# Router by tiles with stationary weights, an earlier first gather, and a last expert loaded in parts, in a float32 decoder trunk on one Trainium2 core

## The chip, the cores and the metric

The kernel runs on one core of one Trainium2 chip. The metric is the time of one execution on the device in microseconds (us); lower is better. All data are float32.

## What is computed

```python
# x: (1, 256, 1024). Layer 0: sliding-window attention and a dense SwiGLU (D_FF 2816).
# Layer 1: pooling mixer, then 8 experts of 3584, of which each token uses 2.
x = x + sliding_window_attention(rms_norm(x, attn_norm), ...)
x = x + swiglu(rms_norm(x, ffn_norm), ffn_w_gate, ffn_w_up, ffn_w_down)
x = x + pooling_mixer(rms_norm(x, pool_norm), pool_w, pool_scale)
t = rms_norm(x, moe_norm)
logits = t @ w_router                       # (256, 8)
top_val, top_idx = lax.top_k(logits, 2)
gates = softmax(top_val)                    # combine[token, expert]
for e in range(8):
    out += combine[:, e:e+1] * ((silu(t @ w_gate[e]) * (t @ w_up[e])) @ w_down[e])
x = x + out
return rms_norm(x, final_norm)
```

## The kernel before, in words

The 256 tokens are two tiles `t` of 128. `xres` holds the residual, `nrm` its normalised copy. Each engine runs its own instruction list in order, and semaphores (`wait_ge`, `then_inc`) tie them together. All weights come through a ring of six SBUF slots of 28 KB per partition; SyncE (SP) issues the loads in order and waits ahead of each one until TensorE has read the slot's old content.

The order around the change is this.

1. **Pooling mixer.** TensorE runs `map_groups(t, half)` (L1281), VectorE adds its result to `xres` (`add_mix`, L832).
2. **Router.** TensorE transposes raw `xres` (`raw_transposes`, L1291) into banks 0 to 3, ScalarE copies these to `rT` (L577), and TensorE multiplies (`logits`, L1304): the 128x128 token block is stationary and only 8 columns, the experts, move. For each tile there are 8 products, which the profile shows as 16 matmul instructions. VectorE copies the logits (L852), takes the top two and builds `mask` (L858). TensorE turns the masks of both tiles into ranks, with `upper` and `ones` as the other operand (L1326 to L1332), VectorE makes `slot` from them (L862, L865) and compares with `iota_f` to get the selection matrix `disp` (`dispatch`, L874). `keep_busy(n)` (L1267) puts in transposes of the identity whose result nobody reads.
3. **First gather.** `gather(0, 0)` (L1335) selects the tokens of expert 0: 16 products of `nrm` by `disp`, 32 instructions, begun when `disp` is there for both tiles. VectorE's `keep_xg` (L880) multiplies the result by the gain, into `xg`.
4. **Flags.** From the counts VectorE ranks the experts by load and writes `flags` (L907 to L930), of which SP, TensorE, ScalarE and VectorE read which expert is next and whether it has over 64 tokens (`ext`, the overflow).
5. **Experts** (`expert`, L1438). Each has 12 chunks of 3.5 MB: gate and up in turns (c = 0 to 7, `gate_up`, L1411, overflow L1392), then four of down (c = 8 to 11, L1503, overflow L1524). The result `y` of an expert is scattered back to the tokens during the next one (`scatter`, L1367), and VectorE adds it to `xres` (L899).
6. **Final.** After expert 7 `final` scatters its `y`, behind a branch on `ext` (L1376: no overflow). ScalarE makes the sum of squares and the root (L507), VectorE multiplies by the gain `final_norm` (L1043, L1051) and by the reciprocal root (L1056, columns 0 to 511; ScalarE L646 has the others), and SP stores each tile (L434).

VectorE's order in the router is: `add_mix` of all halves, `norm(3, t)` (scaling of `nrm`, L657), top two of both tiles, `slot`, `dispatch(0, 0)`, the counts and flags, then `keep_xg(0, 0)`.

Of the kernel before, what the change touches and what calls it, by code (L numbers as in the profile page):

```python
# [20 lines left out]
P = 128  # L21
# [70 lines left out]
def trunk_kernel(nc, x, norm_gains, attn_w_qkv, attn_sinks, attn_w_o, ffn_w_gate, ffn_w_up,  # L92
                 ffn_w_down, pool_w, pool_scale, moe_w_router, moe_w_gate,
                 moe_w_up, moe_w_down, final_norm, out):
    with ExitStack() as ctx:
# [66 lines left out]

        upper = part(arena, 4096, P)
# [22 lines left out]
        lg = sb("lg", [P, T, NE])  # L186
# [22 lines left out]
        full = [sem(f"full{i}") for i in range(SLOTS)]  # L209
        pool_step = sem("pool_step")  # L210
# [39 lines left out]
        poolT_ready = sem("poolT_ready")  # L250
        router_ready = sem("router_ready")
# [3 lines left out]
        mix_done = sem("mix_done")  # L255
        logits_done = sem("logits_done")
# [34 lines left out]
        out_ready = sem("out_ready")  # L291
# [63 lines left out]

        def moe_full(it, c):


            return landed[moe_slot(c)] + 32 * it + 16 * (c // SLOTS + 1)
# [5 lines left out]
        def _(sp):  # L365
# [8 lines left out]
            def load_chunk(it, e, c):  # L374
# [5 lines left out]
                sp.dma_start(ring[s][:, :], w.rearrange("o p n -> (o p) n")).then_inc(full[s], 16)  # L380
# [51 lines left out]
            for t in range(T):  # L432
                sp.wait_ge(out_ready, 2 * t + 2)
                sp.dma_start(out[0].rearrange("(t p) d -> t p d", p=P)[t], out_rows(t)).then_inc(out_sent, 16)  # L434
# [5 lines left out]
        def _(pool):  # L440
# [19 lines left out]
            own.link(nc.gpsimd.tensor_copy(iota_f[:, :], iota_w[:, 0:CAP]))  # L460
# [22 lines left out]
            nc.gpsimd.memset(comb[:, :, NIT:NIT + 1], 0.0).then_inc(zeros_ready, 1)  # L483


            for done, n in ((y_ready, 2), (yx_ready, 2), (sc_ready, 1), (ctr_done, 1), (scat_done, 4), (xadd_done, 8)):
                pool.sem_inc(done, n)


        @block.scalar  # L490
        def _(act):
# [9 lines left out]
            def norm(q, t):  # L501

                if q == 0:
                    act.wait_ge(x_in[t], 16)
                else:
# [65 lines left out]
            for t in range(T):  # L571
                norm(2, t)
            for t in range(T):
                norm(3, t)
                for kh in range(2):
# [3 lines left out]
                                         ACT.Copy).then_inc(rT_ready, 1)  # L579
            preload(ACT.Exp)  # L580
# [56 lines left out]
            with act.If(over > 0):  # L637
                with act.Fori(NE, NIT, 1) as it:
                    expert(it)
            with act.Else():  # L640
                pass
            preload(ACT.Sqrt)
            for t in range(T):
                norm(4, t)
                act.wait_ge(rstd_ready, t + 1)
                nc.scalar.activation(out_rows(t)[:, BANK:D], out_rows(t)[:, BANK:D], ACT.Copy,  # L646
                                     scale=rstd[:, t:t + 1]).then_inc(out_ready, 1)
# [3 lines left out]
        def _(dve):  # L651
# [42 lines left out]
            gained(router[:, :, :], router[:, :, :], 3 * KD, KD).then_inc(router_ready, 1)  # L694
# [150 lines left out]
            norm(3, 1)  # L845
# [3 lines left out]
            cols8 = iota_f[:, 0:NE].rearrange("p (t e) -> p t e", t=1).broadcast_to([P, T, NE])  # L849
            for t in range(T):  # L850
                dve.wait_ge(logits_done, t + 1)
                own.link(nc.vector.tensor_copy(lg[:, t, :], bank[4 + t][:, 0:NE]))  # L852
                own.link(nc.vector.max(top[:, t, :], lg[:, t, :]))
                own.link(nc.vector.max_index(topi[:, t, :], top[:, t, :], lg[:, t, :]))
                own.link(nc.vector.tensor_tensor(
                    pick[:, t, :, :], cols8,
# [3 lines left out]
            dve.wait_ge(mask_ready, 2)  # L860
            dve.wait_ge(rank_done, 1)
            own.link(nc.vector.scalar_tensor_tensor(  # L862
                out=slot[:, :, 0:NE], in0=bank[0][:, 0:T * NE].rearrange("p (t e) -> p t e", t=T),
                scalar=1000.0, in1=mask[:, :, :], op0=ALU.add, op1=ALU.mult))
            own.link(nc.vector.tensor_scalar(slot[:, :, 0:NE], slot[:, :, 0:NE], -1000.0, None, ALU.add))  # L865
# [36 lines left out]
            dispatch(0, 0)  # L902
# [3 lines left out]
            dve.wait_ge(rank_done, 2)  # L906
            own.link(nc.vector.tensor_copy(cnt[:, :], bank[1][:, 0:NE]))  # L907


            own.link(nc.vector.scalar_tensor_tensor(out=key[:, :], in0=iota_f[:, 0:NE], scalar=-1.0 / 16,  # L910
# [691 lines left out]
```

## Time and profile before

| | us |
|---|---|
| median of 3 runs | 1176.99 |
| lowest, highest | 1176.12, 1178.05 |
| profiled execution, device time | 1178.55 |
| its span (first to last instruction) | 1176.6 |
| TensorE busy in the span | 1149.0 (98%) |
| weight loads of TensorE | 554.9 (47%) |
| VectorE, ScalarE, GpSimd busy | 233.5, 129.8, 15.3 |
| DMA, read from HBM | 400.61 MB, mean 341 GB/s |

A time on the left of a row is counted from the span's start. A TensorE busy time is the union of its matmuls; the mean of one instruction includes the time in which it overlaps its neighbours. PEld is the weight load. "PEclk" is the clock that TensorE was granted, 1.00 being 2.4 GHz and 0.50 being 1.2 GHz. "idle before <-X" names what ended the idle time ahead of an instruction. The profiled execution is one execution; 1.95 us of its time lie outside its span.

### The profile page before, as it was taken

The numbers are of one execution on the slowest core, as the hardware profiler recorded it, in microseconds if no ns is written. First come the engines' busy times: TensorE is split into PE (matmuls) and PEld (weight loads), VectorE is DVE, ScalarE is ACT, GpSimd is POOL, SyncE is SP. The second block draws the span as 40 slices with busy tenths as digits, with TensorE's granted clock in tenths as the row PEclk, the third lists the DMA queues.
The fourth block names the chain that finished last, engine by engine and source line by source line (L and its number), as shares of the span: only waits on it lengthen the run. The fifth ranks groups of instructions, "written<-read, shape, count | busy, mean of one in ns | idle before, by whom it ended". The sixth has DMA issues, their size and how long they took to land.

```text
span 1176.6 us, 15165 instructions
## 1 busy us (share of the span) xinstructions
PE 1149.0 (98%) x6492; PEld 554.9 (47%) x6493; DVE 233.5 (20%) x477; ACT 129.8 (11%) x281; POOL 15.3 (1%) x52
## 2 busy tenths in 40 slices
PE   8999999999999999999999999999999999999985
PEld 7647888874483342353333335333333533333331
DVE  3542000046651110110111011011101102111102
ACT  1451000010030110000011000010100001010002
POOL 1300000000000000000000000000000000000000
PEclk9999999999989999999999999999999999999997
DMA  8434036534397999999999999999999999999992
GB/s 313 190 134 189 12 168 254 230 134 149 121 419 320 371 394 373 419 424 433 430 430 429 395 430 432 430 428 429 431 428 432 428 429 429 428 434 426 427 428 97
DMA packets 18838, 402.93 MB, mean 342 GB/s; under 512 B 3264, under 2 KB 3264, under 8 KB 4032
## 3 DMA queue, kind: packets, MB, share of 16 engines
q1 hardware_dynamic: 18752, 401.67, 81.1%
q8 instruction: 68, 1.11, 0.4%
q14 instruction: 18, 0.15, 0.0%
HBM read 400.61 MB, written 1.05 MB: 341 GB/s over the span
## 4 chain that ended last, share of the span: by engine, by line
PE 89%; DMA 7%; DVE 2%; ACT 1%; issue 1%; SPq 0%; DVEq 0%; ACTq 0%
PE bank L1411 32%; PE bank L1503 13%; PE bank L1208 13%; PE bank L1392 8%; PE bank L1234 6%; PE bank L1524 4%; DMA ring<-moe_w_up 3%; DMA ring<-moe_w_down 3%; PE bank L1166 2%; PE bank L1110 2%; PE bank L1371 1%; PE bank L1353 1%; PE bank L1341 1%; PE bank L1376 1%; PE bank L1469 1%; PE bank L1086 1%
## 5 line engine op out<-in xcount | busy, mean ns | idle before, releaser
L1411 PE MATMUL bank<-ring,arena 128*64 128x448 f32 x2048 | 391.3, 540 | 1.4 <-DMA ring<-moe_w_up 1.4
L1411 PEld LDWEIGHTS bank<-ring,arena 128*64 128x64 f32 x2048 | 144.7, 137 | 246.9 <-issue 244.6
L1503 PE MATMUL bank<-ring,arena 128*64 128x512 f32 x896 | 199.0, 599 | 5.8 <-DMA ring<-moe_w_down 3.8
L1208 PE MATMUL bank<-ring 128*128 128x256 f32 (+1 forms) x768 | 152.8, 362 | 0.0
L1208 PEld LDWEIGHTS bank<-ring 128*128 128x128 f32 x768 | 136.0, 190 | 17.0 <-issue 0.5
L1503 PEld LDWEIGHTS bank<-ring,arena 128*64 128x64 f32 x896 | 64.2, 138 | 128.9 <-issue 120.4
L1392 PE MATMUL bank<-ring,arena 128*32 128x448 f32 x1024 | 99.7, 541 | 0.0
L963 DVE TENSOR_TENSOR arena<-bank,arena 128x448 f32<-128x448 f32 x32 | 20.0, 625 | 334.5 <-PE bank L1411 334.5
L1392 PEld LDWEIGHTS bank<-ring,arena 128*32 128x32 f32 x1024 | 31.5, 110 | 66.6 <-issue 66.6
L1013 DVE COPY arena<-bank 64x512 f32<-64x512 f32 x8 | 5.6, 694 | 233.4 <-PE bank L1503 233.4
L1524 PE MATMUL bank<-ring,arena 128*32 128x512 f32 x448 | 51.8, 594 | 0.0
L597 ACT ACTIVATE arena<-bank 128x448 f32<-128x448 f32 x32 | 17.4, 543 | 299.2 <-PE bank L1411 299.2
L1234 PE MATMUL bank<-ring,arena 128*128 128x512 f32 x84 | 37.7, 592 | 0.0
L777 DVE TENSOR_TENSOR arena<-bank,arena 128x256 f32<-128x256 f32 x22 | 9.3, 425 | 132.6 <-ACT arena L566 132.6
L1524 PEld LDWEIGHTS bank<-ring,arena 128*32 128x32 f32 x448 | 14.0, 110 | 36.9 <-issue 36.9
L1110 PE MATMUL bank<-ring 128*64 128x256 f32 x256 | 28.5, 381 | 0.0
L1166 PE MATMUL bank<-ring 128*128 128x512 f32 x64 | 28.5, 595 | 0.0
L1234 PEld LDWEIGHTS bank<-ring,arena 128*128 128x128 f32 x84 | 16.0, 190 | 19.7 <-issue 19.6
L1234 PE MATMUL bank<-ring 128*128 128x512 f32 x54 | 24.3, 592 | 0.0
L566 ACT ACTIVATE arena<-bank 128x256 f32<-128x256 f32 x22 | 8.4, 383 | 141.5 <-PE bank L1208 141.5
L632 ACT ACTIVATE arena<-bank 64x512 f32<-64x512 f32 x8 | 4.7, 590 | 173.1 <-PE bank L1503 173.1
L603 ACT ACTIVATE arena<-bank 64x448 f32<-64x448 f32 x16 | 8.6, 540 | 133.7 <-PE bank L1392 133.7
(187 smaller groups left out, 623.5 us busy)
## 6 DMA issues: line engine op xcount, KB each, us to landing
ring<-moe_w_gate SPq DMA_DIRECT2D x32, 3584.0 KB, 24.5
ring<-moe_w_up SPq DMA_DIRECT2D x32, 3584.0 KB, 27.3
ring<-moe_w_down SPq DMA_DIRECT2D x32, 3584.0 KB, 28.0
ring<-ffn_w_gate SPq DMA_DIRECT2D x2, 3072.0 KB, 10.1
ring<-ffn_w_up SPq DMA_DIRECT2D x2, 3072.0 KB, 10.4
ring<-ffn_w_down SPq DMA_DIRECT2D x2, 3072.0 KB, 14.6
ring<-ffn_w_gate SPq DMA_DIRECT2D x2, 2560.0 KB, 13.6
ring<-ffn_w_up SPq DMA_DIRECT2D x2, 2560.0 KB, 19.2
```

What stands on the lines that cost most here:

```text
L597: nc.scalar.activation(sil[:, j % 2, :], bank[2 * (j % 2)][:, 0:FJ], ACT.Silu).then_inc(sil_ready, 1)
L963: nc.vector.tensor_tensor(hid[:, js], bank[2 * (j % 2) + 1][:, 0:FJ], sil[:, j % 2, :], ALU.mult).then_inc(hid_ready, 1)
L1086: last = mm(bank[7][:, t * KVW:t * KVW + KVW], hT[:, k, t * P:t * P + P], w[:, k, KVW:2 * KVW], start=k == 0, stop=k == KD - 1)
L1110: last = mm(bank[4 + 2 * m + i // 2][64 * b:64 * b + 64, (i % 2) * S:(i % 2) * S + S], w[:, k, c:c + HD], hT[:, k, :], start=k == 0, stop= ...
L1166: last = mm(bank[2 * t + h][:, :], oT[:, 4 * m + i, t * P:t * P + P], w[:, i, h * BANK:h * BANK + BANK], start=m == 0 and i == 0, stop=m = ...
L1208: last = mm(bank[u % 4][:, half * S + ts.start:half * S + ts.stop], w[:, k, f:f + P], hT[:, k, ts], start=k == 0, stop=k == KD - 1)
L1234: return mm(bank[PRODUCT_BANK[i]][:, :], b[lhs], b[rhs], start=p == 0, stop=p == PAIRS - 1)
L1341: last = mm(bank[6 + k // 4][:, (k % 4) * CAP:(k % 4) * CAP + CAP], nrm[:, t, k * P:k * P + P], disp[:, t, side * CAP:side * CAP + CAP], s ...
L1392: last = mm(bank[4 + up][q:q + 32, 0:FJ], xg[:, k, side + BASE:side + CAP], w[:, k, h, :], start=k < 2, stop=k >= KD - 2)
L1411: last = mm(bank[2 * (j % 2) + up][64 * h:64 * h + 64, 0:FJ], xg[:, k, side:side + BASE], w[:, k, h, :], start=k == 0, stop=k == KD - 1)
L1503: last = mm(bank[2][64 * h:64 * h + 64, :], hg[:, i0 + i, half * BASE:half * BASE + BASE], w[:, i, h * BANK:h * BANK + BANK], start=d == 0 ...
L1524: last = mm(bank[3][q:q + 32, :], hgx[:, ii, half * EXT:half * EXT + EXT], w[:, ii % ID, h * BANK:h * BANK + BANK], start=half == 0 and ii ...
```

## The change

- **Router products.** `wide`, the router weights padded to 32 columns per block of 128 rows, is now the stationary operand and the 128 tokens move (`logit_parts`); the four blocks k % 4 go to four groups of 32 PSUM partitions. VectorE copies the 128x128 result to `lT` (`fold_parts`), and one more product by `fold` adds the four groups and turns it back (`logits`). GpSimd builds `wide`'s zeros, `cols8` and `fold` in the beginning.
- **By tiles.** `choose`, `place` and `first_dispatch` run for tile 0 while tile 1's logits are made, ranks go to bank 0 and bank 1 (counts to bank 2), and the gather of expert 0 is cut in two: `first_gather(0, ...)` for tile 0, then tile 1. `iota_f` starts from 1000, so that one instruction for `slot` goes. The logits are read from PSUM, without the copy.
- **nrm of tile 1** is scaled on ScalarE (`nrm1_ready`) and no longer on VectorE; ScalarE does its norm after the four `rT` copies.
- **Order.** `keep_xg(0, 0)` goes ahead of the counts and flags; TensorE waits for `flags_ready` only between the first gate and the overflow.
- **keep_busy.** 3 identity transposes in the router for 14 before, and 6 new ones between the transposes of the two tiles at the very beginning.
- **Loads.** Chunks 9, 10 and 11 of expert 7 are loaded in two DMAs each (columns of i = 0 to 3, then 4 to 6, with semaphores `late_half`).
- **Final.** `scatter` without the branch, on all 128 rows (`y` is zeroed first by GpSimd); `If` and `Else` exchanged, so that the usual case comes first; GpSimd multiplies tile 0 by `final_norm`, VectorE tile 1; ScalarE makes both norms before it scales.

```diff
+                if in_halves(it, c):          # it == NE - 1 and c > 8
+                    at = 4 * D
+                    sp.dma_start(ring[s][:, 0:at], w[:, 0:at]).then_inc(full[s], 16)
+                    sp.dma_start(ring[s][:, at:SLOT], w[:, at:SLOT]).then_inc(late_half[c - 8], 16)
...
+            pool.wait_ge(final_in, 16)
+            pool.wait_ge(final_x, 2)
+            nc.gpsimd.tensor_tensor(out_rows(0), xres[:, 0, :], final_b, ALU.mult).then_inc(out_scaled, 1)
...
+            norm(3, 0)
             for t in range(T):
-                norm(3, t)
                 for kh in range(2):
                     act.wait_ge(tr_done, 4 * T + 2 * t + kh + 1)
...
+            norm(3, 1)
+            act.wait_ge(nrm1_ready, 1)
+            nc.scalar.activation(nrm[:, 1, :], xres[:, 1, :], ACT.Copy,
+                                 scale=rstd[:, 1:2]).then_inc(nrm_ready, 1)
...
             preload(ACT.Sqrt)
             for t in range(T):
                 norm(4, t)
+            for t in range(T):
                 act.wait_ge(rstd_ready, t + 1)
+                if t == 0:
+                    act.wait_ge(out_scaled, 1)
...
+            fold_parts(0)
+            choose(0)
+            fold_parts(1)
+            place(0)
+            first_dispatch(0)
+            dve.wait_ge(std_ready, 3 * T + 2)
+            nc.vector.reciprocal(rstd[:, 1:2], std[:, 1:2]).then_inc(nrm1_ready, 1)
+            choose(1)
+            place(1)
+            first_dispatch(1)
...
-            transposes(0, 0)
+            transposes(0, 0, (0,))
+            for _ in range(6):
+                nc.tensor.transpose(bank[7][:, 0:P], ident[:, :], ident[:, :])
+            transposes(0, 0, (1,))
...
+            def logit_parts(t):
                 for k in range(KD):
                     if k % 4 == 0:
                         pe.wait_ge(rT_ready, 2 * t + k // 4 + 1)
-                    last = mm(bank[4 + t][:, 0:NE], rT[:, k, t * P:t * P + P], router[:, k, :],
-                              start=k == 0, stop=k == KD - 1)
+                    q = 32 * (k % 4)
+                    last = mm(bank[4 + t][q:q + 32, 0:P], wide[:, k, :], rT[:, k, t * P:t * P + P],
+                              start=k < 4, stop=k >= 4)
+                last.then_inc(parts_done, 1)
+
+            def logits(t):
+                pe.wait_ge(lT_ready, t + 1)
+                mm(bank[4 + t][:, P:P + NE], lT[:, t, :], fold, start=True, stop=True).then_inc(logits_done, 1)
...
             map_groups(1, 1)
+            raw_transposes(1, 0)
             pe.wait_ge(router_ready, 1)
             pe.wait_ge(const_ready, 1)
+            logit_parts(0)
+            raw_transposes(1, 1)
             logits(0)
-            raw_transposes(1)
-            keep_busy(4)
-            logits(1)
+            logit_parts(1)
             pe.wait_ge(tri_ready, 1)
             pe.wait_ge(mask_ready, 1)
-            mm(bank[0][:, 0:NE], upper[:, :], mask[:, 0, :], start=True, stop=True)
-            mm(bank[0][:, NE:2 * NE], ones[:, :], mask[:, 0, :], start=True, stop=False)
-            keep_busy(6)
+            mm(bank[0][:, 0:NE], upper[:, :], mask[:, 0, :], start=True, stop=True).then_inc(rank_done, 1)
+            logits(1)
+            keep_busy(3)
+            pe.wait_ge(nrm_ready, 3 * T + 1)
+            pe.wait_ge(disp_part, 1)
+            first_gather(0, range(6))
             pe.wait_ge(mask_ready, 2)
...
+            first_gather(0, range(6, KD))
+            pe.wait_ge(nrm_ready, 3 * T + 2)
+            pe.wait_ge(disp_ready, 1)
+            first_gather(1, range(KD))
...
+                        if i == 4 and in_halves(it, c):
+                            pe.wait_ge(late_half[d], 16)
...
             def final(n):
-                ext = pe.value_load(flags[0:1, n:n + 1], min_val=0, max_val=1)
...
-                scatter(ext, n, 0, 6)
-                scatter(ext, n, 1, 0)
+                for t in range(T):
+                    for h in range(2):
+                        mm(bank[(6, 0)[t] + h][:, :], sc[:, T * h + t, :], y[:, h, :],
+                           start=True, stop=True).then_inc(scat_done, 1)
```

## Rows read from the trace of the kernel before

**Rows 1.** Chain of work that ended last, shares of the span by engine (page).
```profile
PE 89%; DMA 7%; DVE 2%; ACT 1%; issue 1%; SPq 0%; DVEq 0%; ACTq 0%
```

**Rows 2.** Waits of TensorE: total us, times, longest us.
```profile
PE bank L1503 <- DMA ring<-moe_w_down: 3.8, 3, 2.3
PE bank L1411 <- DMA ring<-moe_w_up: 1.4, 1, 1.4
```

**Rows 3.** Windows: length; PE, PEld, DVE, ACT, POOL busy (instructions); PEclk; DMA share; GB/s.
```profile
350.00:470.00 120.00, 120.00 (x806) 43.83 (x804) 17.42 (x40) 11.73 (x21) 0.00 (x0) 1.00 0.89 365
380.00:385.00 5.00, 5.00 (x56) 1.71 (x56) 1.24 (x2) 0.69 (x2) 0.00 (x0) 1.00 0.30 75
700.00:1140.00 440.00, 434.11 (x2582) 164.55 (x2580) 57.66 (x102) 35.44 (x63) 0.00 (x0) 1.00 1.00 430
```

**Rows 4.** Timeline of the router: start us, us, engine, line, operation.
```profile
335.37 1.85 PE L1308 MATMUL bank<-router,arena 128*128 128x8 f32 x16
...
337.07 1.07 PE L1300 MATMUL bank<-ident,xres 128*128 128x128 f32 x8
...
338.00 0.75 DVE L657 TENSOR_SCALAR nrm<-xres,rstd 128x1024 f32<-128x1024 f32 x1
...
338.67 0.16 DVE L852 COPY lg<-bank 128x8 f32<-128x8 f32 x1
...
339.55 0.17 DVE L858 TENSOR_TENSOR mask<-pick 128x8 f32<-128x8 f32 x1
...
343.67 5.95 PE L1341 MATMUL bank<-disp,nrm 128*128 128x96 f32 x32
...
345.31 0.19 DVE L930 CAST flags<-flagf 128x52 int32<-128x52 f32 x1
...
349.55 6.24 PE L1411 MATMUL bank<-ring,arena 128*64 128x448 f32 x32
```

**Rows 5.** Windows at the router and the tail, columns as in the third group.
```profile
338.00:341.50 3.50, 3.50 (x33) 3.22 (x31) 2.50 (x13) 2.31 (x4) 0.00 (x0) 1.00 0.98 414
341.50:348.50 7.00, 7.00 (x34) 7.00 (x35) 3.50 (x23) 1.69 (x3) 0.00 (x0) 0.51 0.98 419
...
8.50:10.00 1.50, 0.01 (x1) 0.01 (x1) 0.98 (x3) 0.42 (x3) 0.00 (x0) 1.00 1.01 426
...
1164.00:1167.50 3.50, 3.50 (x8) 1.03 (x8) 1.29 (x2) 0.12 (x1) 0.00 (x0) 0.52 0.00 0
```

**Rows 6.** Timeline of TensorE over the last expert's down chunks and the scatter.
```profile
1138.29 6.23 PE L1503 MATMUL bank<-ring,arena 128*64 128x512 f32 x28 [1.00 <-DMA ring<-moe_w_down]
1146.80 7.92 PE L1503 MATMUL bank<-ring,arena 128*64 128x512 f32 x28 [2.28 <-DMA ring<-moe_w_down]
1155.27 6.23 PE L1503 MATMUL bank<-ring,arena 128*64 128x512 f32 x28 [0.55 <-DMA ring<-moe_w_down]
1163.96 3.65 PE L1376 MATMUL bank<-arena 64*128 64x512 f32 x8 [2.46 <-issue]
```

**Rows 7.** Timeline of the other engines after the last down chunk.
```profile
1161.55 0.69 DVE L1013 COPY arena<-bank 64x512 f32<-64x512 f32 x1 [30.79 <-PE bank L1503]
...
1167.38 1.06 ACT L507 ACTIVATE nrm<-xres 128x1024 f32<-128x1024 f32 x1 [3.64 <-DVEq L1027]
1167.51 1.23 DVE L1043 TENSOR_TENSOR ring<-xres,ring 128x1024 f32<-128x1024 f32 x1 [0.22 <-DVEq L1027]
...
1168.66 1.28 DVE L899 TENSOR_TENSOR xres<-bank,xres 128x512 f32<-128x512 f32 x2
...
1172.70 0.72 ACT L646 ACTIVATE ring<-ring,rstd 128x512 f32<-128x512 f32 x1 [0.23 <-DVE rstd L1054]
```

**Rows 8.** Groups by form: busy us, mean ns of one; and one row of the timeline.
```profile
L1392 PE MATMUL bank<-ring,arena 128*32 128x448 f32 x1024 | 99.7, 541 | 0.0
...
L475 POOL TENSOR_TENSOR arena<-arena,ident 128x128 f32<-128x128 f32 x8 | 3.6, 456 | 0.7
...
481.07 1.98 PE L1371 MATMUL bank<-arena 128*128 128x512 f32 x4
```

More of the change, by code:

```diff
@@ L160, in trunk_kernel @@
         scale_b = part(ring[1], 4096, D)
+        wide = part(arena, 7680, KD, 32)
+        cols8 = part(arena, 7936, NE)
+        fold = part(arena, 7944, NE)
+        lT = part(arena, 5632, T, P)
         upper = part(arena, 4096, P)
@@ L209, in trunk_kernel @@
         full = [sem(f"full{i}") for i in range(SLOTS)]
+        late_half = [sem(f"late_half{d}") for d in range(4)]
         pool_step = sem("pool_step")
@@ L636, in _ @@
             over = act.value_load(flags[0:1, OVER:OVER + 1], min_val=0, max_val=1)
-            with act.If(over > 0):
+            with act.If(over < 1):
+                pass
+            with act.Else():
                 with act.Fori(NE, NIT, 1) as it:
                     expert(it)
-            with act.Else():
-                pass
             preload(ACT.Sqrt)
@@ L859, in _, with place, first_dispatch @@
                                         ALU.add).then_inc(mask_ready, 1)
[L860 to L865, printed above, removed]
+            def place(t):
+                dve.wait_ge(mask_ready, t + 1)
+                dve.wait_ge(rank_done, t + 1)
+                own.link(nc.vector.scalar_tensor_tensor(
+                    out=slot[:, t, 0:NE], in0=bank[t][:, 0:NE], scalar=1000.0, in1=mask[:, t, :],
+                    op0=ALU.add, op1=ALU.mult))
+            def first_dispatch(t):
+                nc.vector.tensor_scalar(disp[:, t, 0:CAP], iota_f[:, 0:CAP], slot[:, t, 0:1], None,
+                                        ALU.is_equal).then_inc((disp_part, disp_ready)[t], 1)
+            fold_parts(0)
[8 more added lines that the diff above has]
+            first_dispatch(1)
+            dve.wait_ge(nrm1_ready, 1)
             def flag(at, top=1):
@@ L1307, in logits, with first_gather @@
                         pe.wait_ge(rT_ready, 2 * t + k // 4 + 1)
-                    last = mm(bank[4 + t][:, 0:NE], rT[:, k, t * P:t * P + P], router[:, k, :],
-                              start=k == 0, stop=k == KD - 1)
-                last.then_inc(logits_done, 1)
+                    q = 32 * (k % 4)
[5 more added lines that the diff above has]
+                mm(bank[4 + t][:, P:P + NE], lT[:, t, :], fold, start=True, stop=True).then_inc(logits_done, 1)
+            def first_gather(t, ks):
+                for k in ks:
+                    last = mm(bank[6 + k // 4][:, (k % 4) * CAP:(k % 4) * CAP + CAP],
+                              nrm[:, t, k * P:k * P + P], disp[:, t, 0:CAP],
+                              start=t == 0 and k % 4 == 0, stop=t == 1 and k % 4 == 3)
+                    if t == 1 and k % 4 == 3:
+                        last.then_inc(gather_done, 1)
             map_groups(0, 0)
@@ L1413, in gate_up @@
                     last.then_inc(up_done if up else gate_done, 1)
+                    if apart and not up:
+                        pe.wait_ge(flags_ready, 1)
+                        ext = flag(it + 1)
                     if apart:
```

153 lines of the change are left out of this document (85 added, 68 removed).

## The prediction

> **What bounds the kernel now.** I read the chain of work first, to see which engine carries the end: TensorE holds 89% of it [rows 1]. Then TensorE's waits, to see whether it is TensorE's speed or its data: only four waits name a weight load, 5.2 us together [rows 2]. Three of them are at the last three down chunks [rows 6]. So up to there TensorE's own work sets the pace, and any time saved ahead of the experts would pass on, if the loads can follow. Whether they can is what the windows show. From 700 on the DMA is full (share 1.00, 430 GB/s), but between 350 and 470 it is busy only 0.89 of the time, and from 380 to 385 only 0.30 [rows 3]: there the loads wait for TensorE to give slots back. A tenth of 120 us is some 13 us of idle loading, more than the router can save; so if TensorE enters expert 0 earlier by D, the slots are given back D earlier, and the full stretch behind begins and ends D earlier. Last I read the timelines of the router and of the tail, where nearly every step waits for the one before.
>
> **Part 1, the router and first gather.** Before, this stretch runs from 335.37 (first logits product) to 349.55 (first gate product), 14.2 us [rows 4]. I lay out the new order with the rows' prices.
> - Tile 1's first four transposes: half of 1.07 for eight, 0.55 [rows 4], to 335.9.
> - `logit_parts(0)`: 16 instructions. The nearest rows bound it. As before, 16 in 1.85 [rows 4]; or as the overflow products, which also use 32 columns of weights and four column groups: 99.7 us for 1024 of 448 columns is 0.097 each, which for 128 columns is 0.028, so 0.45 for 16 [rows 8]. I take 0.6, near the second, since it has the same shape of weights; done at 336.5.
> - Result to VectorE 0.2, `lT` copy 0.3 (twice the 0.16 of the 8-column copy [rows 4], for 128 columns), the fold product 0.25 (two of the 16 in 1.85) and 0.2 back: 337.4.
> - Top two: before from 338.67 to 339.72 with the copy (0.2), so 0.85 without [rows 4]. The mask of tile 0 is there at 338.3 and no longer at 339.72. VectorE had begun late because it was scaling `nrm` of tile 1 (0.75 at 338.00 [rows 4]); that goes to ScalarE, at 1.06 as its pass over 1024 columns [rows 7], beside TensorE's work.
> - Tile 1: its second transposes end near 337.0 on TensorE, ScalarE copies, `logit_parts(1)` ends at 338.3, the copy at 338.65 and the product at 339.1. Meanwhile the rank product of tile 0 (0.25) and its `slot` and `disp` (0.2 each with hand-over) give `disp_part` at 339.3.
> - The 12 instructions of `first_gather(0)` then fill the time in which VectorE takes tile 1's top two (339.55 to 340.4). At 2.4 GHz one costs about 0.12, as the transposes, which load the same 128x128 weights (1.07 for eight [rows 4]): 1.4, to 340.8. The four rank and count products take 1.0, four more gather instructions 0.5: 342.3. `disp` of tile 1 (341.9) and `nrm` of tile 1 (about 341) are ready. Its 16 instructions take 1.9: 344.2.
> So D is 5.3 if the clock stays up. I take 4.8, with 0.5 for hand-overs that the list leaves out. The other end: TensorE's granted clock was 0.51 from 341.5 to 348.5, after a stretch (338.0 to 341.5) with 8-column products, waits and identity transposes [rows 5]. That is why the gather took 5.95 [rows 4] where 32 at 0.12 would be 3.8. If the new order also falls to 1.2 GHz at about 340, its 32 gather instructions cost 3.8 more in the worst case, and D is 1.5 to 2.1. A D above 6 would need the parts and the hand-overs to be free.
> What covers the rest: the flags move behind `keep_xg(0, 0)`; before, they stood at 345.5, 4 us ahead of the gate [rows 4]. Now they come about 2.3 us of small VectorE instructions after the last `xg` (344.9), at 347.3; behind TensorE's wait for them is queued only the overflow of the first gate, which begins after the gate's 6.24 us [rows 4], at 350.5. So nothing; each us beyond 3 would cost one. ScalarE's Exp table now loads after its `nrm`; its result is needed for `comb`, which no engine reads before the first down chunks. GpSimd's new instructions at the start are over long before 26 us, the zeroing of `y` before expert 0 ends. All these I cost at nothing.
> The six identity transposes at the start lie in a gap of TensorE (8.5 to 10.0: 0.01 us busy) in which the clock stayed 1.00 [rows 5]: they take 0.7 of the 1.5 and gain nothing; 0, at worst 0.2 lost.
>
> **Part 2, the last chunks in two parts.** Each of chunks 9, 10 and 11 made TensorE wait (1.00, 2.28, 0.55), and the landings of the last two are 8.47 apart [rows 6]. Four sevenths of a chunk would land 3/7 of that, 3.6 us, before the rest. At the last landing (1155.27) TensorE today begins all 6.23 us; then it would have only 3/7 of it, 2.67, provided that the first part is done: it lands at 1151.6 and takes 3.56, done at 1155.2. So 3.5 us, of the 6.23 whole. Ends: 3.56 above; below 1.8, if TensorE's clock falls in its new wait of 2 us ahead of the last chunk, as after the 2.28 wait, when the same 28 instructions took 7.92 and not 6.23 [rows 6]; and 0, if both parts land together (a rival).
>
> **Part 3, after the last product.** The copy of `y` ends at 1162.24; the scatter begins 1.72 later, behind the branch [rows 6, 7], and runs at clock 0.52 [rows 5]: the first add could begin at 1166.0, 2.0 us later. All is over with ScalarE's last scaling at 1173.42 [rows 7], 11.2 after `y`. New, from `y` = 0: the branch on TensorE goes, but VectorE's own branch ahead of `yx_ready` stays: 0.4 (between 0.1 and 1.0). Full-row products cost 1.98 for two at 2.4 GHz, 0.87 each and 0.25 for the end [rows 8]; an add takes 0.64 (1.28 for two [rows 7]). Tile 0 complete at 0.4 + 1.98 + 0.1 + 0.64 = 3.1; tile 1 at 3.1 + 1.75 = 4.85. ScalarE: square of tile 1 with root, 1.5 (1.06 and two small ones), 6.4; VectorE's multiplication of tile 1, 1.23 [rows 7], 6.1. Two scalings of 0.72 [rows 7] behind each other: 7.9. GpSimd has 3.1 to about 6.4 for tile 0: two SBUF inputs, 128 columns in 0.456 [rows 8], so between eight times that, 3.6, and as VectorE, 1.23; I take 2.5, done at 5.6, which covers it. The two output DMAs now follow each other within 0.7, which costs 0.3 more. Sum 11.2 - 8.2 = 3.0; ends 1.5 and 3.8.
> The Trainium skill, "SBUF — State Buffer", section "Who interferes with whom", has a rule against this very pair: a VectorE instruction with two SBUF inputs and a GpSimd instruction that reads SBUF exclude each other, and the later one waits until the other is over. No row here shows such a pair of length, so it is a rival below.
>
> **The sum.** 4.8 + 3.5 + 3.0 = 11.3 us. Made against the profiled execution, 1178.55 (span 1176.6 and 1.95 outside), this gives 1167.3; that execution is 1.56 above the median of 1176.99, from which it would be 1165.7. As part of its excess may be its own low clock, I take the middle, 1166.5; own range 1164 to 1168.5.
>
> **The rivals.**
> - *The gather still runs at 1.2 GHz.* For: few columns move between 337 and 339.4 in the new list too. Against: the parts move 128 columns where 8 moved, and the gather begins 4 us sooner. D falls by 2.7 to 2.1: 1169.2. Chance 0.20.
> - *VectorE and GpSimd exclude each other in the tail.* VectorE's multiplication of tile 1 (from 4.85) waits for GpSimd's (until 5.6, or 6.7 at the slow end) and both scalings are late by 0.7 to 1.8: 1167.8. By the skill's rule this is what happens. Chance 0.12.
> - *Parts of a chunk land together*, since the queue works on both at once: part 2 gives nothing, 1170.0. Against: landings 8.47 apart [rows 6] look like one chunk after the other. Chance 0.06.
> - *The loads can't follow*, and TensorE only waits longer at 1138: D is lost, 1171.3. Against: the idle loading of [rows 3]. Chance 0.05.
> - *Two of these, or unlisted costs, eat all*: within 0.2% of before. Chance 0.03.
> - *Slower: GpSimd's multiplication of tile 0.* ScalarE's and VectorE's scaling and both stores wait for it. With duration p the end is 3.1 + p + 1.44 after `y`; before it was 11.2, and the other parts save 8.3, so it must pass 15 us to break even and 17.4 to be slower by 0.2%, five times the slow end. At 19 us: 1181. Chance 0.02, and with other surprises of that sign 0.03.
>
> **How the numbers follow.** Forecast 0.51, rivals as given. The likeliest gives 1166.5. The range takes in the clock and port rivals and the low ends of parts 2 and 3 (1169.2 + 1.5), and above the best sum, 6 + 3.56 + 3.8 = 13.4 from 1176.99: 1163.5 to 1171.0. Under 0.2% (2.4 us), this kernel's measurement can't tell a change from none. Faster holds in all cases but the last two: 0.94, same 0.03, slower 0.03.
>
> **What would show it.** First gate product near 344.7 after a span start like before's, with the clock at 1.00 over the gather (right) or 0.5 (first rival). Waits of TensorE at chunks 9 and 10 gone, and the last product 2.7 us after the last landing. The scatter within 0.5 us of `y` at clock 1.00, VectorE's multiplication of tile 1 at 1.23 and not later than the last add. DMA share from 350 to 470 up from 0.89. Wrong if the last landing isn't earlier by D although the first gate product is.

## The result, and the profile after

| | before | after |
|---|---|---|
| median, same session (6 runs each) | 1177.24 us | 1167.38 us |
| lowest to highest | 1176.12 to 1178.05 | 1166.09 to 1169.33 |
| profiled execution; its span | 1178.55; 1176.6 | 1166.09; 1164.3 |
| TensorE busy; its mean granted clock | 1149.0; 0.992 | 1142.2; 0.999 |

The ratio is 0.9918 (95% interval 0.9905 to 0.9931): 9.9 us faster, 0.9 above the forecast. The kernel was measured twice more beside experiments, 1166.48 and 1166.87.

The head of the page of after, and its chain of work:

```profile
PE 1142.2 (98%) x6491; PEld 548.8 (47%) x6492; DVE 232.4 (20%) x475; ACT 131.0 (11%) x282; POOL 19.8 (2%) x60
...
PE 90%; DMA 7%; DVE 2%; ACT 1%; issue 0%; SPq 0%; ACTq 0%; DVEq 0%
```

TensorE is busy 6.8 us less, with nearly the same number of matmuls (6491 for 6492). By stretches (columns as in [rows 3]), the router of before, that of after, and for comparison the old router in an execution in which the clock didn't fall (the kernel with the parts alone, below):

```profile
335.37:349.55 14.18, 14.18 (x98) 13.81 (x96) 6.85 (x38) 5.68 (x10) 0.00 (x0) 0.76 1.00 430
334.86:343.64 8.78, 8.40 (x91) 7.08 (x89) 4.42 (x21) 6.85 (x11) 0.00 (x0) 1.00 1.00 430
335.51:347.13 11.62, 11.26 (x97) 10.60 (x96) 6.98 (x39) 5.68 (x10) 0.00 (x0) 1.00 1.01 433
```

Of the 5.8 us less in the router, 2.9 (14.18 for 11.26) go with the clock and 2.9 (11.26 for 8.40) with shorter and fewer instructions: the logits products and the identity transposes. Another 1.7 is the clock in the last chunks, and the start has 0.7 more. So about 4.6 of it all is clock. "issue" has gone from 1% [rows 1] to 0%; it turns out below to be the most instructive figure of this case.

TensorE's waits for loads (total, times, longest), against [rows 2]:

```profile
PE bank L1592 <- DMA ring<-moe_w_down: 1.8, 1, 1.8
...
PE bank L1494 <- DMA ring<-moe_w_up: 1.1, 1, 1.1
```

Two of the three waits for down chunks are gone. The windows (PE, PEld, DVE, ACT, POOL busy, clock, DMA share, GB/s), against [rows 3] and [rows 5]:

```profile
350.00:470.00 120.00, 120.00 (x806) 43.96 (x800) 16.62 (x30) 12.19 (x22) 0.00 (x0) 1.00 0.93 382
380.00:385.00 5.00, 5.00 (x32) 1.78 (x26) 1.69 (x4) 0.54 (x1) 0.00 (x0) 1.00 1.00 430
700.00:1140.00 440.00, 435.34 (x2586) 164.75 (x2584) 56.88 (x98) 34.90 (x62) 0.00 (x0) 1.00 1.00 429
...
341.50:345.00 3.50, 3.50 (x28) 2.67 (x29) 1.95 (x9) 1.85 (x4) 0.00 (x0) 1.00 1.10 475
```

The loads follow: the idle part of the loading from 350 to 470 has shrunk from 0.11 to 0.07, and the last load lets TensorE go on at 1148.82 where it was 1155.27 [rows 6], 6.45 us earlier, when the first gate product is 5.91 earlier. In the last line the clock is 1.00 where it was 0.51 [rows 5].

TensorE in the router (start us, us, engine, line, operation), against [rows 4]:

```profile
334.86 0.60 PE L1359 MATMUL bank<-ident,xres 128*128 128x128 f32 x4
335.39 0.65 PE L1370 MATMUL bank<-arena 128*32 128x128 f32 x16
...
339.03 1.55 PE L1380 MATMUL bank<-disp,nrm 128*128 128x96 f32 x12
...
341.26 2.45 PE L1380 MATMUL bank<-disp,nrm 128*128 128x96 f32 x20
343.64 6.23 PE L1494 MATMUL bank<-ring,arena 128*64 128x448 f32 x32
```

The stretch starts 0.51 earlier than before (334.86 for 335.37), since the second tile of `x` landed earlier in this execution (ScalarE begins its square at 6.95 for 7.47); the first gate product comes at 343.64 for 349.55. So D is 5.91 - 0.51 = 5.40. The gather takes 1.55 + 2.45 = 4.0 for 5.95.

The last chunks and the tail, against [rows 6, 7]:

```profile
1131.10 12.24 PE L1592 MATMUL bank<-ring,arena 128*64 128x512 f32 x56
...
1145.15 6.47 PE L1592 MATMUL bank<-ring,arena 128*64 128x512 f32 x28 [1.81 <-DMA ring<-moe_w_down]
...
1151.66 0.69 DVE L1074 COPY arena<-bank 64x512 f32<-64x512 f32 x1 [27.03 <-PE bank L1592]
...
1152.62 3.67 PE L1631 MATMUL bank<-arena 128*128 128x512 f32 x8 [1.00 <-DVE arena L1074]
...
1155.45 2.35 POOL L520 TENSOR_TENSOR ring<-xres,ring 128x1024 f32<-128x1024 f32 x1 [827.17 <-DVE xres L1089]
...
1157.13 1.76 DVE L1106 TENSOR_TENSOR ring<-xres,ring 128x1024 f32<-128x1024 f32 x1
...
1159.12 1.33 ACT L687 ACTIVATE ring<-ring,rstd 128x512 f32<-128x512 f32 x2 [0.60 <-DVE rstd L1109]
```

Chunks 9 and 10 run as one block of 56. `y` is in SBUF at 1152.35, 9.89 earlier than before; 5.91 of that is the earlier first gate, so the last chunks gave 3.98. From `y` to the end of the span it is 11.95 for 14.36, so the tail gave 2.4. All together 0.51 + 5.40 + 3.98 + 2.41 = 12.3, the difference of the spans.

### The profile page after: what moved, and what is told of

The parts are those of the page before. It is cut to its first block, busy times and chain, and to the rows that moved or that the text cites. A ratio compares the mean times of both kernels' runs of the same rounds, so it can differ in the third digit from the quotient of the medians.

```text
span 1164.3 us, 15176 instructions
## 1 busy us (share of the span) xinstructions
PE 1142.2 (98%) x6491; PEld 548.8 (47%) x6492; DVE 232.4 (20%) x475; ACT 131.0 (11%) x282; POOL 19.8 (2%) x60
## 4 chain that ended last, share of the span: by engine, by line
PE 90%; DMA 7%; DVE 2%; ACT 1%; issue 0%; SPq 0%; ACTq 0%; DVEq 0%
PE bank L1494 32%; PE bank L1592 13%; PE bank L1268 13%; PE bank L1475 8%; PE bank L1294 6%; PE bank L1613 4%; DMA ring<-moe_w_up 3%; DMA ring<-moe_w_down 3%; PE bank L1226 2%; PE bank L1170 2%; PE bank L1454 1%; PE bank L1436 1%; PE bank L1556 1%; PE bank L1146 1%; PE bank L1346 1%; PE bank L1158 1%
```

## The experiments

Twelve runs followed, two of them of the changed kernel again. Three groups of them each shared their runs of before, whose medians were 1177.35 (A), 1176.44 (B) and 1176.75 (C).

### The same kernel again (A and C)

> The changed kernel itself, beside the next three. Its six runs fall in two groups, about 1166.3 and 1168.5. Theory: the second group is runs in which TensorE's clock fell to 1.2 GHz once in the router or the tail (mean clock 0.997 for 0.999). Then the profile, if it is of the second group, shows one stretch at 0.5 of some 3 to 7 us in the router or at the last chunks. Rival: the groups differ by the landing of loads; then the stretches are alike and the waits for loads differ. Time 1166 to 1169.5.

> The changed kernel once more, beside the next three, for their comparison: 1166 to 1169, median 1166.8.

Measured 1166.48 (1166.02 to 1167.83, ratio 0.9905, 0.9889 to 0.9922) and 1166.87 (1164.56 to 1168.38, ratio 0.9919, 0.9906 to 0.9933). The first gate product is at 343.3 to 344.4 in all nine profiles of after and of the kernels below that keep its router, and the gather takes 1.55 + 2.45 in each. The first rival of the prediction doesn't happen. The runs spread over 4 us all the same. The mean clock orders the six runs of the result (1166.1 to 1166.6 at 0.998 to 0.999, 1168.2 to 1169.3 at 0.996 to 0.997), but not the four of group A: 1166.02 came at 0.997 and 1167.83 at 0.999.

### The early gather undone (A)

```diff
-            pe.wait_ge(nrm_ready, 3 * T + 1)
-            pe.wait_ge(disp_part, 1)
-            first_gather(0, range(6))
             pe.wait_ge(mask_ready, 2)
...
-            first_gather(0, range(6, KD))
+            pe.wait_ge(nrm_ready, 3 * T + 1)
+            pe.wait_ge(disp_part, 1)
             pe.wait_ge(nrm_ready, 3 * T + 2)
             pe.wait_ge(disp_ready, 1)
+            first_gather(0, range(KD))
             first_gather(1, range(KD))
```

> The products of the first gather for tile 0 wait until tile 1's selection is there too; router products, masks and all else as changed. Theory (the early start is worth the 16 instructions at 2.4 GHz, about 0.12 each): 1.9 us slower than the changed kernel, the clock stays at 1.00. Rival (the early gather's main worth is that it keeps the clock up): the clock falls to 0.5 over the gather and it is 4 to 6 us slower.

Measured 1169.96 (1168.05 to 1171.41, ratio 0.9928, 0.9912 to 0.9945), 3.5 slower than after beside it. TensorE's timeline, and a window:

```profile
339.99 0.39 PE L1406 MATMUL bank<-mask,arena 128*128 128x8 f32 x2 [0.86 <-DVE mask L904]
...
341.33 6.78 PE L1380 MATMUL bank<-disp,nrm 128*128 128x96 f32 x32 [0.17 <-DVE disp L915]
348.04 4.35 PE L1493 MATMUL bank<-ring,arena 128*64 128x448 f32 x22
...
340.00:345.00 5.00, 4.83 (x25) 4.76 (x26) 0.67 (x4) 3.43 (x6) 0.00 (x0) 0.58 0.98 424
```

So the early gather fills the wait for tile 1's selection (TensorE waits 0.86 here), and by this profile it also keeps the clock: with a wait and short products in its place the mean clock from 340 to 345 is 0.58 and the 32 gather instructions take 6.78 for 4.0. That is one profile against nine with the early gather in which the clock held. The first gate product is 4.2 us later than in after, with the 0.21 by which this stretch starts later left out. The rival of the prediction was a real one; of its two arguments against it, the wider moves are here too and didn't suffice, and the earlier gather is the one that is left.

### The clock in the old router (A)

The old order, with each product moving 128 columns (the 8 router columns repeated 16 times).

```diff
-                    last = mm(bank[4 + t][:, 0:NE], rT[:, k, t * P:t * P + P], router[:, k, :],
+                    last = mm(bank[4 + t][:, 0:P].rearrange("p (a e) -> p a e", e=NE),
+                              rT[:, k, t * P:t * P + P],
+                              router[:, k:k + 1, :].broadcast_to([P, P // NE, NE]),
                               start=k == 0, stop=k == KD - 1)
```

> The kernel before, in which the router products move 128 columns (the 8 router columns repeated 16 times) and not 8; the logits are the same, the instructions as many. Weight loads take 0.12 us each, so the products should take as long as before. Theory (the clock fell because few columns moved between 335 and 341): the clock stays at 1.00 to 349, the 32 gather instructions take 3.8 us and not 5.95, first gate product 2.5 to 3.5 us earlier, 2.5 to 3.5 us faster than before. Rival (the clock fell from the waits of the two-tile chain): it falls at the same place, time within 0.5 us of before.

Measured 1176.53 (1173.9 to 1177.7, ratio 0.9986, 0.9977 to 0.9996). Timeline of TensorE:

```profile
337.21 1.95 PE L1308 MATMUL bank<-router,arena 128*128 128x128 f32 x16
...
344.91 3.81 PE L1343 MATMUL bank<-disp,nrm 128*128 128x96 f32 x32
349.00 3.23 PE L1413 MATMUL bank<-ring,arena 128*64 128x448 f32 x16 [0.28 <-issue]
```

The stretch from the first logits product to the first gate takes 11.8 for 14.2 [rows 4], the gather 3.81 for 5.95. That part is as expected, but the time fell by only 0.8 by the medians and 1.6 by the ratio. Two things in the traces fit that. In this execution the clock fell at the start instead (`L1086` took 5.32 for 3.69, clock 0.67 from 10 to 14), so the stretch itself began 1.84 later than in the profile of before (1.6 for the clock, the rest for a later tile of `x`). And the fall in the gather isn't there in every execution of the old router: the kernel with the parts alone, below, has that router unchanged, and its gather too took 3.81:

```profile
343.05 3.81 PE L1352 MATMUL bank<-disp,nrm 128*128 128x96 f32 x32
347.13 5.11 PE L1422 MATMUL bank<-ring,arena 128*64 128x448 f32 x26 [0.27 <-issue]
```

So [rows 4] and [rows 5] showed one of two courses of the old router, the one with the fall, and this experiment doesn't show that wide moves keep the clock up.

### The start's identity transposes undone (B)

```diff
-            for _ in range(6):
-                nc.tensor.transpose(bank[7][:, 0:P], ident[:, :], ident[:, :])
```

> The changed kernel without the six identity transposes between the first two tiles' transposes. The prediction gave them nothing to save, because the clock stayed up in the kernel before's trace. But in a later trace of a kernel without them, the clock fell to 1.2 GHz behind that gap, and the first 16 value products took 5.32 us and not 3.69. Theory A (the prediction's): no difference, within 0.3 us. Theory B (they keep the clock up in some runs): 1.6 us slower in a part of the runs, so the runs fall in two groups, and the median is 0.5 to 1.6 us slower; the profile shows 3.7 or 5.3 us for the 16 products.

Measured 1166.83 (1165.82 to 1167.71, ratio 0.9917, 0.99 to 0.9934): no difference from after. TensorE idled 2.27 us ahead of the transposes of tile 1 and kept its clock (3.69 us for the 16 products that follow); with the same gap the kernel above lost it. What they are worth is then a matter of which course an execution takes; on the time of after it can't be seen. The trace has a second lesson, in expert 6 (counted from 0):

```profile
961.05 7.93 PE L1492 MATMUL bank<-ring,arena 128*64 128x448 f32 x32 [2.27 <-DMA ring<-moe_w_up]
...
1134.93 18.25 PE L1590 MATMUL bank<-ring,arena 128*64 128x512 f32 x84
```

A wait of 2.27 for a load is followed by 7.93 where 6.2 is usual; the wait's length doesn't decide it, for waits of 2.28 (the kernel with the clock kept, at 963.34) and 2.54 (the one above, at 1145.34) were followed by 6.23. TensorE is then late: its first gate product was 0.7 later than in the profile of after, its transposes ahead of the last down chunks begin 3.8 later (1125.90 for 1122.07). But it has no wait for the last chunks, and `y` is only 1.6 later: of the 3.1 lost in the middle 0.8 is left. The loads set the end, and TensorE's delays in the middle are mostly taken up by waits that go.

### The last chunks whole (A)

```diff
         def in_halves(it, c):
-            return isinstance(it, int) and it == NE - 1 and c > 8
+            return False
```

> The last three chunks whole again, all else as changed. Theory (parts land one after the other, and TensorE has only the second part left at the last landing): 3.5 us slower than the changed kernel, 1.8 to 4, and TensorE waits 1.0, 2.3 and 0.6 at chunks 9, 10 and 11 again. Rival (the parts bring nothing, the tail was faster for the clock alone): within 1 us of the changed kernel.

Measured 1170.75 (1169.6 to 1173.36, ratio 0.9946, 0.9927 to 0.9965), 4.3 slower than after beside it; 3.3 by the spans of the profiles.

```profile
1139.43 6.23 PE L1592 MATMUL bank<-ring,arena 128*64 128x512 f32 x28 [1.95 <-DMA ring<-moe_w_down]
1147.78 7.92 PE L1592 MATMUL bank<-ring,arena 128*64 128x512 f32 x28 [2.12 <-DMA ring<-moe_w_down]
```

Both waits are back, and behind the second the last chunk takes 7.92 (clock 0.57 from 1148 to 1152). In after and its repetitions the wait ahead of the last chunk is 1.7 to 1.9 and its clock holds. So the parts take 3.4 off the work behind the last landing (in after it is 2.80, from 1148.82 to 1151.62, for 6.23), and 1.7 more where a whole chunk meets a fallen clock, as in this profile.

### Finer parts, and filled waits (B and C)

```diff
+LAST_PARTS = ((3, 5), (5, 6), (6, 7))
...
-                if in_halves(it, c):
+                if in_halves(it, c) and c == PER_IT - 1:
+                    sp.dma_start(ring[s][:, 0:3 * D], w[:, 0:3 * D]).then_inc(full[s], 16)
+                    for j, (a, b) in enumerate(LAST_PARTS):
+                        sp.dma_start(ring[s][:, a * D:b * D], w[:, a * D:b * D]).then_inc(late_last[j], 16)
...
```

The last chunk comes in four DMAs, for i = 0 to 2, then 3 and 4, 5, 6.

> A version that may beat both: the last chunk in four DMAs (3, 2, 1 and 1 of its 7 blocks) and not two, all else as changed. Theory (at the end TensorE has left what came with the last landing, and the loads set the pace there): one block, 0.89 us, is left and not three, 2.67, so 1.5 to 1.8 us faster than the changed kernel. Rival (4 KB rows load slower, or the clock falls in the more frequent waits): 0 to 0.8 faster, or slower by up to 1.

Measured 1165.56 (1164.85 to 1167.13, ratio 0.9911, 0.9888 to 0.9934), 0.9 to 1.8 under the three medians of after, not surely a difference.

```profile
1144.79 6.23 PE L1602 MATMUL bank<-ring,arena 128*64 128x512 f32 x28 [0.89 <-DMA ring<-moe_w_down]
```

The first gate product of this execution is at 344.23, as in the two repetitions of after (344.32 and 344.23), so these are what to compare with. Their last chunk begins at 1146.01 and 1145.83, this one 1.0 to 1.2 earlier; it runs its 6.23 without a stop, and `y` is there at 1151.75 for 1153.22 and 1153.04, 1.3 to 1.5 earlier. That is a little less than the 1.5 to 1.8 expected. With the first part there, TensorE's own 6.2 us set the end, not the later landings.

The same with 12 identity transposes ahead of the last chunk and ahead of expert 6's first up chunk, where the fall of the clock had been seen:

> A version that may beat both: the last chunk in four DMAs, and 12 identity transposes ahead of each of the two waits for loads that the changed kernel still has (first up chunk of the expert before the last, and the last chunk). Theory (in a part of the runs the clock falls behind such a wait, as in a trace where it was 2.27 us long and the next 32 products took 7.93 and not 6.23): the slower runs go, none is over 1167.5, median 1165.2 or less, 1.2 to 2 us under the changed kernel. Rival (the runs differ by when loads land, not by the clock): as far apart as before, median about 1165.6 as with the four DMAs alone.

Measured 1165.72 (1165.4 to 1168.34, ratio 0.9914, 0.9901 to 0.9927). The last chunk begins without a wait and takes 6.23, expert 6's first up chunk waits 0.81 and takes 6.23, and the runs spread over 2.9 us still. So the spread isn't these two falls of the clock alone. The trace fits that it is when loads land, but nothing here shows that.

### The tail: GpSimd's share and the inner branch (B)

```diff
-            nc.gpsimd.tensor_tensor(out_rows(0), xres[:, 0, :], final_b, ALU.mult).then_inc(out_scaled, 1)
+            nc.vector.tensor_tensor(out_rows(0), xres[:, 0, :], final_b, ALU.mult).then_inc(out_scaled, 1)
```

> VectorE multiplies both tiles by the final gain, GpSimd does nothing in the tail. In the changed kernel VectorE's multiplication of tile 1 took 1.76 us and ended 1.1 us after GpSimd's. Theory (the two exclude each other, one waits): both rows are 1.23 here, VectorE starts the first right after the last add, and the kernel is 0.5 to 0.9 us slower as two rows of 1.23 take the place of one of 1.76. Rival (the 1.76 has another cause, such as ScalarE's reading of the same rows): the rows stay at 1.5 to 1.8 and it is 1.5 to 2 us slower.

Measured 1166.71 (1166.33 to 1168.45, ratio 0.9922, 0.9899 to 0.9945).

```profile
1156.87 1.23 DVE L1103 TENSOR_TENSOR ring<-xres,ring 128x1024 f32<-128x1024 f32 x1
...
1158.02 1.22 DVE L1104 TENSOR_TENSOR ring<-xres,ring 128x1024 f32<-128x1024 f32 x1
```

And the old scatter of half the rows behind its branch on `ext`, in the new tail:

```diff
             def final(n):
+                ext = pe.value_load(flags[0:1, n:n + 1], min_val=0, max_val=1)
...
-                for t in range(T):
-                    for h in range(2):
-                        mm(bank[(6, 0)[t] + h][:, :], sc[:, T * h + t, :], y[:, h, :], ...)
+                scatter(ext, n, 0, 6)
+                scatter(ext, n, 1, 0)
```

> The last scatter again behind the branch, on 64 rows for each half, all else as changed. Theory (the prediction's term: the branch costs what the full rows don't): 1.0 to 1.4 us slower. Rival (a branch costs 0.6 to 0.9 when the clock is up, and two products on half rows run side by side, 1.06 for two and not 1.75, which gives most of it back): 0 to 0.5 us slower.

Measured 1166.74 (1165.83 to 1167.93, ratio 0.992, 0.9897 to 0.9943).

```profile
1152.87 1.99 PE L1459 MATMUL bank<-arena 64*128 64x512 f32 x8 [1.28 <-DVE arena L1074]
...
1155.55 2.36 POOL L520 TENSOR_TENSOR ring<-xres,ring 128x1024 f32<-128x1024 f32 x1 [827.06 <-DVE xres L1089]
...
1156.70 2.29 DVE L1106 TENSOR_TENSOR ring<-xres,ring 128x1024 f32<-128x1024 f32 x1
```

Two things follow. VectorE and GpSimd do exclude each other: the same VectorE instruction takes 1.22 and 1.23 with GpSimd idle, 1.76 in after and 2.29 here, where it started 0.53 sooner against GpSimd; in after it ends 1.09 behind GpSimd's end (1158.89 and 1157.80), here 1.08 (1158.99 and 1157.91). That VectorE waits for the whole of a GpSimd instruction that was first is the rule of the Trainium skill, "SBUF — State Buffer", section "Who interferes with whom". These traces agree to within 0.15 us (the end 1.09 and 1.08 behind GpSimd's for a whole 1.23), and in after it costs 0.53. Even so GpSimd's share is worth a little in the traces: VectorE alone ends 7.14 behind `y`, with GpSimd's help 6.54. The times can't tell the two kernels apart.

And the inner branch costs next to nothing: the scatter begins 0.55 behind `y` with it, 0.27 without, and half as many rows take half the time (1.99 for 3.67). VectorE can so begin its multiplication 4.38 behind `y` for 4.78, but it then waits the longer for GpSimd and ends 6.67 behind `y` for 6.54. The prediction had named this branch as the gain. It wasn't.

### The parts alone, and all of it but the order of code (C)

These ask for the change's terms one by one on the kernel before: the loads in parts alone, then these with the wide logits products and the start's transposes.

> The kernel before with one part of the change alone: chunks 9, 10 and 11 of the last expert in two DMAs. Theory (as predicted, 3/7 of a chunk's landing time, 3.6, and in some runs the 1.7 of a clock that no longer falls): 3.5 to 5 us faster than before. Rival (the gain in the changed kernel came from meeting the new tail): 0 to 2 us faster.

Measured 1175.91 (1172.66 to 1176.83, ratio 0.9988, 0.9977 to 0.9999).

> The kernel before with only what keeps the clock up or splits loads: router products that move 128 columns, six identity transposes at the start, and the chunks in two DMAs; router order, gather and tail are those of before. Theory (the clock and the split loads are worth more than the new order): 2.7 for the gather at full clock, 0.5 to 1.6 at the start and 3.5 to 5 for the loads, 6.7 to 8.5 us faster than before, 1168 to 1170; what is left to the changed kernel, 2 to 3 us, is the new order of the router. Rival (the order is worth most): 3.5 to 5.5 faster only, 1171 or more.

Measured 1174.30 (1171.19 to 1175.37, ratio 0.9978, 0.9967 to 0.9988). So the parts bring 0.8 here by the medians (1.4 by the ratio, whose interval goes from 0.1 to 2.7), where taking them from after costs 4.3; and all three bring 2.45 (2.6 by the ratio), well under what was expected. The timelines of the first, and one row of the second:

```profile
1134.44 12.24 PE L1516 MATMUL bank<-ring,arena 128*64 128x512 f32 x56
1148.33 6.48 PE L1516 MATMUL bank<-ring,arena 128*64 128x512 f32 x28 [1.65 <-DMA ring<-moe_w_down]
1159.17 3.12 PE L1387 MATMUL bank<-arena 64*128 64x512 f32 x8 [4.36 <-issue]
```

```profile
1160.77 3.78 PE L1392 MATMUL bank<-arena 64*128 64x512 f32 x8 [4.24 <-issue]
```

The parts work as in after: chunks 9 and 10 in one block, the last chunk in 6.48. But then the scatter waits 4.36 and 4.24 for "issue", where it was 2.46 in the profile of before [rows 6]; in after it waits 1.00, and that for VectorE. In the chain of work that is 3.61 us of issue behind VectorE's copy of `y`:

```profile
1154.86 0.70 DVE arena L1024
1155.56 3.61 issue
1159.17 1.45 PE bank L1387 x4
```

The DMA queues point to what it waits for. Queue q8 carries blocks of 16 KB marked "instruction", 68 of them in an execution; for which engine a block is they don't say. Here are the packets that begin between the end of `y` and the scatter, in the kernel with the parts alone, and in the same place in after (1150.3 to 1153.5):

```profile
DMA packets 2, 0.02 MB, mean 9 GB/s; under 512 B 0, under 2 KB 0, under 8 KB 0
...
q8 instruction: 1, 0.02, 2.2%
```

```profile
DMA packets 0, 0.00 MB, mean 0 GB/s; under 512 B 0, under 2 KB 0, under 8 KB 0
```

The starts of q8's packets at the end of each trace, in us:

| kernel | last load lets TensorE go on | q8 packets begin | scatter begins | from first packet to scatter |
|---|---|---|---|---|
| before | 1155.27 | 1158.34, 1159.39, 1163.38 | 1163.96 | 5.62 |
| before, wide products | 1153.84 | 1157.63, 1158.69, 1162.87 | 1163.39 | 5.76 |
| before, parts | 1152.01 | 1153.35, 1154.44, 1158.96 | 1159.17 | 5.82 |
| before, parts, clock kept | 1153.73 | 1155.07, 1156.14, 1160.25 | 1160.77 | 5.70 |
| after | 1148.82 | 1150.17, then 1153.62 | 1152.62 | 2.45 |
| after, inner branch back | 1148.79 | 1150.18, then 1154.25 | 1152.87 | 2.69 |

In all four with the old order of code three blocks of instructions come one after the other, and the scatter begins 0.21 to 0.58 after the third begins. By their recorded ends the third ends 0.65 to 0.79 behind the scatter's start, which is the lag with which the last packet of the weights ends behind the product that waits for it too (0.71 to 0.78 in the four): that fits a scatter that starts when the block is there. In both with the new order the scatter needs no further block. So the old "issue" reads as a chain of instruction loads with a length of its own, 5.6 to 5.8 us from its first packet, and no fixed toll behind `y`. The less TensorE has to do meanwhile, the more of it shows: with whole chunks at full clock the first packet comes 3.07 behind the last landing and the scatter 3.07 + 5.62 = 8.69 behind it; with parts it is 1.34 + 5.82 = 7.16. The parts can give 1.5 there, not 3.6. In after the scatter comes 3.80 behind the last landing.

What makes the third load is most likely the jump; no run shows it by itself. The old code is `If(over > 0)` with the loop over overflow experts, and the usual case in the `Else` behind it; the new one has the usual case first. The inner branch on `ext` is excluded by the kernel above that has it and no third load; it has the old scatter too, so that at its end TensorE's code differs from the old one in the exchange and in the order of two waits alone. VectorE's and ScalarE's code behind the experts differs as well. The Trainium skill, "Runtime: NRT & Kernel Launch", section "Instruction fetch mechanics", says that a taken branch to code outside the blocks at hand forces a fetch of the target's block before execution goes on. The traces fit it, at 4.36 us of idle TensorE in the clearest case. Open is what the exchange of `If` and `Else` brings by itself: on the old kernel it wasn't tried alone.

This also makes the sums meet. From the kernel with parts and clock kept to after, the spans differ by 9.2 (1173.5 and 1164.3): 4.9 is the earlier last landing, 3.2 the scatter behind it (7.04 and 3.80), 1.1 the rest of the tail.

## Why the prediction was right, and where not

The total, 11.3 us by the sum, was 12.3 in the profiles and 9.9 in the medians. The first two parts came about as argued; that the third fits is luck, as its last point says. Each of the parts, by the profiles:

- **Part 1: listed 5.3, taken 4.8, measured 5.40.** Right. The list held nearly line by line: the first parts in 0.65 for 0.6, tile 0's mask at 337.80 and, less the 0.5 of the earlier start, as forecast for 338.3. The deduction of 0.5 for hand-overs wasn't needed. D is the difference to an execution of before in which the clock had fallen; to one in which it hadn't (first logits product at 335.51, first gate at 347.13) it is 2.8. That is at least part of why the medians differ by less than the profiles.
- **The first rival, the clock falling in the gather (0.20).** Didn't happen in nine profiles, and happened in the one in which the early gather was taken out. The argument against it, wider moves, was the weaker half of the reason: the undone gather kept these, and lost the clock.
- **The loads follow.** Right: 5.91 earlier at the first gate, 6.45 at the last landing, share 0.93.
- **The covers.** Right: the flags are there at 346.48, 3.3 ahead of the overflow products at 349.80. The start's transposes gained nothing on the time of after, as costed.
- **Part 2: 3.5, measured 3.98 in the trace and 4.3 by undoing it.** Right; the waits of chunks 9 and 10 are gone and the clock stayed up in the last one. That the parts land one after the other was right too (third rival). What the term hid is that it isn't a number of its own: without part 3 it was 0.8 in the medians, 1.4 by the ratio.
- **Part 3: 3.0, measured 2.4.** The steps were near (scatter at 0.27 for 0.4 behind `y`, tile 0 at 2.95 for 3.1, tile 1 at 4.67 for 4.85, GpSimd 2.35 for 2.5), and two were short: the exclusion of VectorE and GpSimd, put at a chance of 0.12, came true at 0.53, under the 0.7 to 1.8 of the rival since the overlap was short; and the output DMAs cost 0.67 more than before (3.85 from ScalarE's end to the span's end, before 3.18), not 0.3.
- **The step that failed** is the reading of the 1.72 between `y` and the scatter as the cost of the branch on `ext`, gone with that branch. The branch costs 0.3. By the queues the 1.72 was the visible end of a chain of instruction loads, and in the two old kernels with the parts it grew to 3.6 and 3.5. The two errors, a term for the inner branch that wasn't there and a term missing for what went with the outer one, cancelled by luck: the sum counted 1.3 for it, by the traces the new order of code is worth 1.5 without the parts (1.72 for 0.27) and 3.2 to 3.4 with them.

## What to carry to other kernels

An "issue" ahead of the first instruction behind a branch can be a chain of its own that starts well before it, so look at the instruction packets there: if it is one, try the usual case of the branch in line, directly behind the work, before you shorten that work, or the gain turns into a longer "issue". Fill a wait on the path with real work that is ready, as a part of the gather here: it saves the wait, and here it also kept the clock for what came behind, which was the larger part. And undo a part of a change from the finished kernel and also do it alone on the old one; here that gave 4.3 and 0.8 (by the ratio 1.4) for the same edit, and only the difference led to the cause.

## What was not expected of the hardware

- Three blocks of 16 KB of instructions, 5.6 to 5.8 us from the first packet to the start of the scatter, in four profiles with the usual case in the `Else` at the end of the kernel; in the two with the usual case first only the first of these blocks comes ahead of the scatter. That the branch is what makes the third is argued, not shown.
- TensorE's clock can fall or not in the same place of the same code: the old router's gather took 5.95 in one execution and 3.81 in another, and a gap of 2.2 to 2.3 us at the start was followed by 5.32 or 3.69 us for the same products. Waits of 2.12 to 2.28 for a load were followed by 7.9 where 6.2 is usual (four rows), waits of 2.28 and 2.54 were not.
- Late work in the middle isn't late work at the end while loads set the end: 3.1 us lost between the first gate and 1125.90 became 0.8 at `y`.
- The executions of one kernel differ by up to 4 us (1164.56 to 1168.38), and the mean clock orders them in one group of runs and not in another; the cause is open. It isn't the identity transposes at the start, nor the two clock falls that filling the waits took away.
